# Four weight subtractions of the output projection, moved from VectorE to GpSimd behind its others

## What is computed

```python
for l in range(DEPTH):                                  # DEPTH = 2
    proj = x @ w_in[l]                                  # (512, 1024) @ (1024, 2208)
    ...
    y_a = mla_attention(q_lat, kv_lat, k_rope, ...)     # 4 heads x 4 blocks of 128 queries, dense softmax
    y_b = sc_b * depthwise_conv(sc_c * sc_h, sconv_w[l])
    y_c = conformer_conv(cf_a, cf_g, ...)               # 31 taps, LayerNorm, swish
    y_d = window_gqa(gq_q, gq_k, gq_v, sink[l], ...)    # |i - j| <= 128
    mix = jnp.concatenate([y_a, y_b, y_c, y_d], axis=-1) @ w_out[l]
    x = layer_norm(DEEPNORM_ALPHA * x + mix, ln1_g[l], ln1_b[l])
    moe = expert_choice_moe(x, w_router[l], ...)
    x = layer_norm(DEEPNORM_ALPHA * x + moe, ln2_g[l], ln2_b[l])
```

## Time and profile before

| | us |
|---|---|
| median of 3 runs | 1472.83 |
| lowest and highest run | 1471.87 and 1474.85 |
| the profiled execution's own time | 1471.98 |
| its span, from the first to the last instruction | 1470.2 |
| VectorE busy | 496.2 (34%) |
| GpSimd busy | 105.8 (7%) |

### The profile page before, as it was taken

The page is one execution under the profiler, slowest core; times in us unless marked ns, Lnnn a source line. Parts: engine busy times, 40 slices in busy tenths (PEclk is TensorE's granted clock), DMA queues, the critical chain, the costliest instruction groups (busy, mean ns, idle before and its releaser), DMA issues.

```text
span 1470.2 us, 15583 instructions
## 1 busy us (share of the span) xinstructions
PE 1365.1 (93%) x6372; PEld 711.5 (48%) x6372; DVE 496.2 (34%) x1001; ACT 293.1 (20%) x517; POOL 105.8 (7%) x86
## 2 busy tenths in 40 slices
PE   6999999899999999989889998999999999999894
PEld 5766578444334334333467575774343343343332
DVE  6775745311111111110549467261201201201205
ACT  4236630010001001000043457111100000000000
POOL 2320000000000000000133200000000000000001
PEclk9999999999999999999999999999999999999997
DMA  9100353999999999999950012469999999999993
GB/s 377 70 1 1 144 202 150 381 429 416 427 427 429 427 427 427 426 428 427 421 232 0 0 58 100 193 255 388 429 414 428 428 428 427 427 425 429 427 427 163
DMA packets 44405, 459.94 MB, mean 313 GB/s; under 512 B 7856, under 2 KB 8624, under 8 KB 14640
## 3 DMA queue, kind: packets, MB, share of 16 engines
q1 hardware_dynamic: 34416, 436.88, 70.8%
q10 hardware_dynamic: 6752, 10.54, 2.0%
q0 software_dynamic: 3168, 11.54, 1.9%
HBM read 450.55 MB, written 8.39 MB: 312 GB/s over the span
## 4 chain that ended last, share of the span: by engine, by line
PE 75%; DMA 12%; DVE 5%; issue 3%; ACT 3%; ACTq 1%; SPq 0%; DVEq 0%; POOLq 0%
PE bank L914 24%; PE bank L937 13%; PE bank L534 11%; DMA ring<-w_moe 10%; PE bank L881 8%; PE bank L791 2%; PE bank L795 2%; PE bank L794 2%; DMA wr<-w_router 2%; PE bank L489 2%; PE bank L852 1%; PE bank L679 1%; PE bank L959 1%; PE bank L869 1%; PE bank L567 1%
## 5 line engine op out<-in xcount | busy, mean ns | idle before, releaser
L914 PE MATMUL bank<-ring,work 128*64 128x512 f32 x1632 | 357.3, 594 | 13.0 <-issue 8.8
L914 PEld LDWEIGHTS bank<-ring,work 128*64 128x64 f32 x1632 | 134.0, 137 | 222.0 <-issue 201.1
L937 PE MATMUL bank<-ring,w_up 128*64 128x512 f32 x800 | 180.4, 600 | 14.5 <-ACT w_up L1834 9.3
L1512 DVE TENSOR_TENSOR work<-work,bank 128x512 f32<-128x512 f32 x32 | 22.0, 688 | 473.1 <-PE bank L914 472.3
L1531 DVE TENSOR_TENSOR X<-X,bank 128x512 f32<-128x512 f32 x112 | 77.1, 688 | 251.4 <-PE bank L881 251.4
L881 PE MATMUL bank<-work,cst 128*128 128x512 f32 x240 | 116.3, 618 | 9.7 <-ACT work L1855 9.7
L937 PEld LDWEIGHTS bank<-ring,w_up 128*64 128x64 f32 x800 | 63.0, 138 | 121.7 <-issue 106.2
L914 PE MATMUL bank<-work 128*64 128x512 f32 x416 | 92.4, 593 | 1.5 <-issue 1.5
L534 PE MATMUL bank<-x_hi,w_hi 128*128 128x512 f32 x288 | 79.2, 420 | 7.8 <-ACT w_hi L1602 4.1
L881 PEld LDWEIGHTS bank<-work,cst 128*128 128x128 f32 x240 | 38.6, 189 | 87.3 <-DVE X L1531 36.7
L1151 DVE SCALAR_TENSOR_TENSOR bank<-X,par,bank 128x512 f32<-128x512 f32 x120 | 79.9, 748 | 0.9 <-DVE ring L1125 0.9
(11 more groups left out here) (225 smaller groups left out, 1513.7 us busy)
## 6 DMA issues: line engine op xcount, KB each, us to landing
ring<-w_moe SPq DMA_DIRECT2D x146, 2048.0 KB, 25.5
work<-w_moe SPq DMA_DIRECT2D x36, 2048.0 KB, 21.2
ring<-w_moe SPq DMA_DIRECT2D x20, 1024.0 KB, 8.4
ring<-w_in SPq DMA_DIRECT2D x18, 1024.0 KB, 15.7
ring<-w_out SPq DMA_DIRECT2D x8, 1024.0 KB, 29.7
work<-ln SPq DMA_DIRECT2D x4, 1024.0 KB, 16.8
x_rows<-X ACTq DMA_DIRECT2D x8, 512.0 KB, 6.1
out<-X POOLq DMA_DIRECT2D x8, 512.0 KB, 6.5
```

The costliest lines, as they stand in the source:

```text
L914: ins = mm(B((kind, pair, n))[64 * e:64 * e + 64, :], xsT[:, k, 64 * e:64 * e + 64], w[:, e, n * 512:(n + 1) * 512], start=(k == 0), stop= ...
L937: ins = mm(B(("O", pair, n))[64 * e:64 * e + 64, :], hidT[:, k, 64 * e:64 * e + 64], w[:, i, e], start=(k == 0), stop=(k == KD - 1))
L1512: nc.vector.tensor_tensor(hid[:, cols], hid[:, cols], B(("U", pair, n))[:, :], ALU.mult)\
```

## The change

The four subtractions of `wout_lower` leave VectorE in each layer, and the function with them. GpSimd does the same four behind its seven of `w_low` and ahead of the deviations of the first LayerNorm. Each waits for ScalarE's high part, as before. What remains on VectorE keeps its order. TensorE, ScalarE and SyncE are not changed.

```diff
@@ on VectorE
-                def wout_lower(n):
-                    j = OUT_TURN[n]
-                    v.wait_ge(wout_hi_ready, at(lay, 4, n + 1))
-                    nc.vector.tensor_tensor(wout_low[j], ring[:, OUT_RAW[j]], wout_hi[j].bitcast(F32), ALU.subtract)\
-                        .then_inc(wout_lo_ready, 1)
...
                 d_max(1)
-                wout_lower(0)
                 d_norm(1)
...
                 d_max(2)
-                wout_lower(1)
                 d_norm(2)
...
                     a_norm(i)
-                    if i in (2, 7):
-                        wout_lower(2 + i // 7)
                     if i in (4, 5, 8):
@@ on GpSimd
                 for n in range(1, IN_SLOTS - 1):
                     w_low(n)
 
+                for n in range(4):
+                    j = OUT_TURN[n]
+                    hold(wout_hi_ready, at(lay, 4, n + 1))
+                    tt(wout_low[j], ring[:, OUT_RAW[j]], wout_hi[j].bitcast(F32), ALU.subtract).then_inc(wout_lo_ready, 1)
+
                 for t in range(NT):
                     inverse_deviation(lay, t, 0)
```

## The result

| | us |
|---|---|
| before, median with the later runs on the same chip | 1473.3 |
| after, median of 4 runs | 1501.47 |
| after, lowest and highest run | 1494.07 and 1503.07 |
| after, the profiled execution and its span | 1500.59 and 1498.5 |
| ratio after to before, 95% interval | 1.0183 [1.0167, 1.0200] |

The forecast was 1484.0 (1474 to 1488). The direction is right, the size is not: 28.2 us were lost, not 11.2.

What follows compares the result with a forecast made beforehand. TensorE was taken to set the pace, with group A's attention ring waiting on VectorE's normalising; per layer 4.8 us of hold plus 0.8 of clock, twice, 11.2 us on 1472.83, gave 1484.0 us, range 1474 to 1488.

Runs made afterwards that it cites:

- warm_last_two: Changed kernel with only the third and fourth subtraction on GpSimd, plus three unread TensorE matmuls ahead of turning tiles 3 and 6 each: 1481.73 us, ratio 1.0070.
- scores_later: Changed kernel with only the first and second subtraction on GpSimd, and TensorE's eight filling matmuls moved ahead of block 2's third and fourth head scores: 1482.14 us.

## What to carry to other kernels

An instruction that moves to an idle GpSimd may cost VectorE its whole duration. Write down every instruction of VectorE from SBUF to SBUF that stands within that duration, and start GpSimd behind the last one that somebody waits for. For each held instruction ask two questions, who reads what it writes, and who waits for the buffer that it, or what is queued behind it, was going to free; the second is often due earlier. And price a wait of TensorE with the clock behind it: here 4.2 us of hold became 5.6 to 7.2.

## What was not expected of the hardware

- The length of a wait doesn't tell whether the clock falls behind it. It stayed at 1.00 behind 1.17 us at tile 3 in the kernel before, in warm_last_two behind 1.61 us at 187.68 (188 to 192 us: 1.00), and in the changed kernel behind 2.76 us at 195.37; it was 0.82 behind 1.40 us in scores_later and 0.68 behind 3.26 us at 933.68. Unread matmuls in its place kept it at 1.00 three times out of three.
- Even an instruction of 128x4 elements is held: 1.41 us instead of 0.16 at 128.56 us in the changed kernel, beside GpSimd's subtraction of 125.38 to 129.96.
- With pieces of 128 columns both engines pay: beside them VectorE's normalising takes 0.71 to 0.74 us from tile 5 on instead of 0.49 (tiles 3 and 4 took 0.49 and 0.56), and GpSimd's subtraction up to 9.09 us instead of 4.52.
